# Lagging low-part products behind a norm, and a compression on both weight halves at once, in a two-block decoder on one core

## The reference, cut to what matters

```python
def rmsnorm(t, g):
    tf = tf * lax.rsqrt(jnp.mean(tf * tf, axis=-1, keepdims=True) + NORM_EPS)
...
h = rmsnorm(x, norm_mix[i]) * (1.0 + sc1) + sh1      # then h @ wqkv
h2 = rmsnorm(x, norm_ffn[i]) * (1.0 + sc2) + sh2     # then h2 @ ffn_up
...
def nsa_compress(k, pos_emb, w1, b1, w2, b2):
    nc = (T - NSA_CMP_LEN) // NSA_CMP_STRIDE + 1          # 15 blocks
    blocks = k[:, idx] + pos_emb
    flat = blocks.reshape(B, nc, NSA_CMP_LEN * hd)        # 15 x 2048
    return jax.nn.silu(flat @ w1 + b1) @ w2 + b2          # w1: 2048 x 128
```

## Time and profile before

| what | value |
|---|---|
| time, median of 3 runs | 1620.4 us (1619.64 to 1622.11) |
| the profiled execution's own time | 1614.25 us |
| its span, first to last instruction | 1612.1 us |
| granted TensorE clock, mean | 0.996 |
| PE, PEld busy | 98%, 83% |
| DVE, ACT, POOL busy | 59%, 48%, 34% |
| instructions | 24595 |
| matmul records of L731, one and two columns | 84 and 32 |
| DMA | 249.26 MB, 155 GB/s on average |

### The profile page before, as it was taken

The page is one execution under the profiler, slowest core; times in us unless marked ns, Lnnn a source line. Parts: engine busy times, 40 slices in busy tenths (PEclk is TensorE's granted clock), DMA queues, the critical chain, the costliest instruction groups (busy, mean ns, idle before and its releaser), DMA issues.

```text
span 1612.1 us, 24595 instructions
## 1 busy us (share of the span) xinstructions
PE 1584.4 (98%) x9838; PEld 1339.2 (83%) x9838; DVE 949.9 (59%) x1485; ACT 767.5 (48%) x1410; POOL 548.8 (34%) x358
## 2 busy tenths in 40 slices
PE   8999999999999999999999999999999999999998
PEld 5778557778887888879767999999999989999987
DVE  4334485555564653343275888658776567768545
ACT  5323585444322443243274755445544555564454
POOL 2224243322211222123172111016334567533564
PEclk9999999999999999999999999999999999999999
DMA  9264500434174222364314654445534544533451
GB/s 394 83 250 186 228 9 27 183 138 164 48 282 165 83 76 81 140 209 157 104 28 163 238 187 168 169 170 183 182 131 158 183 160 170 185 128 134 180 203 58
DMA packets 52464, 249.26 MB, mean 155 GB/s; under 512 B 20608, under 2 KB 20736, under 8 KB 25856
## 3 DMA queue, kind: packets, MB, share of 16 engines
q1 hardware_dynamic: 43600, 243.90, 41.9%
q10 hardware_dynamic: 8752, 3.80, 1.0%
HBM read 246.63 MB, written 1.05 MB: 154 GB/s over the span
## 4 chain that ended last, share of the span: by engine, by line
PE 89%; DVE 6%; ACT 2%; issue 1%; DMA 1%; POOL 0%; SPq 0%; ACTq 0%; POOLq 0%; DVEq 0%
PE psq L551 14%; PE psq L553 14%; PE psq L552 14%; PE psq L965 7%; PE ps L551 6%; PE ps L553 6%; PE ps L552 6%; PE psq L966 4%; PE ps L965 3%; PE ps L565 2%; PE ps L966 1%; DVE WL L533 1%; PE psq L1373 1%; PE ps L1401 1%; DMA RAW<-wstream 1%
## 5 line engine op out<-in xcount | busy, mean ns | idle before, releaser
L533 POOL TENSOR_TENSOR WL<-RAW,WH 128x1024 fp32r<-128x1024 f32 (+2 forms) x116 | 304.4, 2626 | 504.5 <-ACT WH L523 493.4
L533 DVE TENSOR_TENSOR WL<-RAW,WH 128x1024 fp32r<-128x1024 f32 (+3 forms) x264 | 329.2, 1272 | 235.6 <-ACT WH L523 235.4
L523 ACT ACTIVATE WH<-RAW 128x1024 fp32r<-128x1024 f32 (+2 forms) x380 | 361.0, 1001 | 156.2 <-DMA RAW<-wstream 92.5
L551 PE MATMUL psq<-NHL,WH 128*128 128x256 f32 (+1 forms) x1260 | 410.2, 326 | 3.3 <-POOL NHL L869 1.8
L553 PE MATMUL psq<-NHL,WL 128*128 128x256 f32 (+1 forms) x1260 | 404.3, 321 | 0.0
L552 PE MATMUL psq<-NHL,WH 128*128 128x256 f32 (+1 forms) x1260 | 404.2, 321 | 0.0
L551 PEld LDWEIGHTS psq<-NHL,WH 128*128 128x128 f32 x1260 | 239.9, 190 | 32.4 <-issue 7.6
L553 PEld LDWEIGHTS psq<-NHL,WL 128*128 128x128 f32 x1260 | 239.9, 190 | 17.8
L552 PEld LDWEIGHTS psq<-NHL,WH 128*128 128x128 f32 x1260 | 240.0, 191 | 16.6
L965 PE MATMUL psq<-NHL,WH 128*128 128x512 f32 x416 | 148.6, 400 | 0.0
L551 PE MATMUL ps<-NHL,WH 128*128 128x256 f32 (+1 forms) x368 | 122.1, 332 | 0.0
(11 more groups left out here) (398 smaller groups left out, 2871.0 us busy)
## 6 DMA issues: line engine op xcount, KB each, us to landing
RAW<-wstream SPq DMA_DIRECT2D x196, 1024.0 KB, 4.9
RAW<-wstream SPq DMA_DIRECT2D x32, 704.0 KB, 4.0
K<-first SPq DMA_DIRECT2D x4, 1024.0 KB, 17.1
X<-xin SPq DMA_DIRECT2D x2, 1024.0 KB, 6.3
V<-first SPq DMA_DIRECT2D x2, 1024.0 KB, 19.2
Q<-first SPq DMA_DIRECT2D x2, 1024.0 KB, 25.4
BR<-rpb ACTq DMA_DIRECT2D x8, 256.0 KB, 7.9
BR<-rpb SPq DMA_DIRECT2D x8, 256.0 KB, 8.6
```

What stands on the lines that cost most here:

```text
L523: e.activation(WH[:, u % 3, a:z], RAW[:, v % 3, a:z], ACT.Copy).then_inc(w_hi, 1)
L533: e.tensor_tensor(WL[:, u % 3, a:z], RAW[:, v % 3, a:z], WH[:, u % 3, a:z].bitcast(F32), ALU.subtract).then_inc(w_lo_p if pool else w_lo_v, 1)
L551: e.matmul(o, lh, rh, start=start, stop=False)
```

## The change

The sums over squares stream 64 equal columns (32 of each kind in the double norm) into 64 columns of NB, and dve_mean reads one of them. pe_high_first goes through all k: high products of tile k, then the low product of tile k-1; it replaces the abreast branch of pe_wide and the call of pe_tiles. In dve_head the split for "kf" moves ahead of the memset. WH and WL become two halves of one tensor, so that pe_compress_up can stream 256 columns, 128 high and 128 low, in one matmul; ACT copies 256 columns, and pe_compress_sum adds both halves. The computed values are the same sums in another order.

```diff
-        WH = sb("WH", [P, 3, UNIT], F32R)
-        WL = sb("WL", [P, 3, UNIT], F32R)
+        WHL = sb("WHL", [P, 2, 3, UNIT], F32R)
+        WH, WL = WHL[:, 0, :, :], WHL[:, 1, :, :]
...
-            width = 2 if n == 5 else 1
+            if n == 5:
+                kinds = GSQ[:, m, :].unsqueeze(2).to_broadcast([P, 2, 32])
+            else:
+                kinds = ONE.to_broadcast([P, 64])
             for q in range(NORM_T[n] // P):
-                mm = e.matmul(NB[:, width * q:width * q + width], t[:, q * P:q * P + P], GSQ[:, m, :] if n == 5 else ONE,
+                mm = e.matmul(NB[:, 64 * q:64 * q + 64], t[:, q * P:q * P + P], kinds,
                               start=first and q == 0, stop=m == DT - 1, skip_group_check=True)
...
         def pe_high_first(e, n, key, outs, T, shared):
             v, wh, wl = weights(key)
-            wait_weights(e, v, 0)
-            e.wait_ge(n_hi, split_base(n) + NORM_T[n] // 256)
-            for j, o in enumerate(outs):
-                w = slice(P * j, P * j + P)
-                e.matmul(o, wh[:, 0, w], NH[:, 0, 0:T], start=j == 0 or not shared, stop=False, skip_group_check=shared)
-                e.matmul(o, wl[:, 0, w], NH[:, 0, 0:T], start=False, stop=False, skip_group_check=shared)
-            pe_wait_norm(e, n, 0)
-            for j, o in enumerate(outs):
-                e.matmul(o, wh[:, 0, P * j:P * j + P], NL[:, 0, 0:T], start=False, stop=False, skip_group_check=shared)
+            H, base = NORM_T[n] // 256, split_base(n)
+            for k in range(DT + 1):
+                if k < DT:
+                    wait_weights(e, v, k)
+                    e.wait_ge(n_hi, base + H * k + H)
+                    for j, o in enumerate(outs):
+                        w = slice(P * j, P * j + P)
+                        e.matmul(o, wh[:, k, w], NH[:, k, 0:T], start=k == 0 and (j == 0 or not shared), stop=False,
+                                 skip_group_check=shared)
+                        e.matmul(o, wl[:, k, w], NH[:, k, 0:T], start=False, stop=False, skip_group_check=shared)
+                if k:
+                    pe_wait_norm(e, n, k - 1)
+                    for j, o in enumerate(outs):
+                        mm = e.matmul(o, wh[:, k - 1, P * j:P * j + P], NL[:, k - 1, 0:T], start=False, stop=k == DT,
+                                      skip_group_check=shared)
+                        if k == DT and (not shared or j == 1):
+                            mm.then_inc(gemm, 1)
...
+            lo_prep(e, l, "kf", False)
             e.memset(CM[:, 0:384].bitcast(U32), 0).then_inc(cm_zero, 1)
             dve_turn_product(e, l, 1)
-            lo_prep(e, l, "kf", False)
             dve_turn_sum(e, l, 1, KN[:, :, :])
...
-                v, wh, wl = weights(("cmp", l, kind))
+                v = UNIT_OF[("cmp", l, kind)]
+                both = WHL[:, :, SPLIT_AT[v] % 3, :].rearrange("p s (k n) -> p s k n", k=16)
                 for k in range(16):
-                    lhs = FHL[:, 512 * kind + 32 * k:512 * kind + 32 * k + P]
                     wait_weights(e, v, k)
-                    e.matmul(bank[6 + kind][:, 0:P], lhs, wh[:, k, :], start=k == 0, stop=False)
-                    mm = e.matmul(bank[6 + kind][:, 0:P], lhs, wl[:, k, :], start=False, stop=k == 15)
+                    mm = e.matmul(bank[6 + kind][:, 0:256], FHL[:, 512 * kind + 32 * k:512 * kind + 32 * k + P],
+                                  both[:, :, k, :], start=k == 0, stop=k == 15)
...
-                e.matmul(bank[6][:, 256 + 16 * kind:272 + 16 * kind], TMP[0:32, 3 + kind, 0:P],
-                         CONST[0:32, CO["sum16"]:CO["sum16"] + 16], start=True, stop=True).then_inc(cmp_mm, 1)
+                for half in range(2):
+                    mm = e.matmul(bank[6][:, 256 + 16 * kind:272 + 16 * kind],
+                                  TMP[0:32, 3 + kind, P * half:P * half + P],
+                                  CONST[0:32, CO["sum16"]:CO["sum16"] + 16], start=half == 0, stop=half == 1)
+                mm.then_inc(cmp_mm, 1)
```

More of the change, by code:

```diff
@@ L779, in dve_mean @@
                 for kind in range(2):
-                    mm = e.tensor_scalar(MS[:, 2 * kind:2 * kind + 2], NB[:, 0:4].rearrange("p (q s) -> p s q", s=2)[:, kind, :],
+                    mm = e.tensor_scalar(MS[:, 2 * kind:2 * kind + 2], NB[:, 32 * kind:32 * kind + 128:64],
                                          1.0 / D, EPS * EPS if kind == 0 else EPS, ALU.mult, ALU.add)
@@ L783, in dve_mean @@
                 return
-            e.tensor_scalar(MS[:, 0:nt], NB[:, 0:nt], 1.0 / D, EPS, ALU.mult, ALU.add).then_inc(ms_done, 1)
+            sums = NB[:, 0:nt] if n == 0 else NB[:, 0:64 * nt:64]
+            e.tensor_scalar(MS[:, 0:nt], sums, 1.0 / D, EPS, ALU.mult, ALU.add).then_inc(ms_done, 1)
         def rs_columns(n):
@@ L903, in pe_high_first, with pe_wide @@
             v, wh, wl = weights(key)
-            wait_weights(e, v, 0)
-            e.wait_ge(n_hi, split_base(n) + NORM_T[n] // 256)
-            for j, o in enumerate(outs):
-                w = slice(P * j, P * j + P)
-                e.matmul(o, wh[:, 0, w], NH[:, 0, 0:T], start=j == 0 or not shared, stop=False, skip_group_check=shared)
-                e.matmul(o, wl[:, 0, w], NH[:, 0, 0:T], start=False, stop=False, skip_group_check=shared)
-            pe_wait_norm(e, n, 0)
-            for j, o in enumerate(outs):
-                e.matmul(o, wh[:, 0, P * j:P * j + P], NL[:, 0, 0:T], start=False, stop=False, skip_group_check=shared)
-        def pe_wide(e, key, outs, T, xh, xl, wait_x, abreast=False):
+            H, base = NORM_T[n] // 256, split_base(n)
[15 more added lines that the diff above has]
+                            mm.then_inc(gemm, 1)
+        def pe_wide(e, key, outs, T, xh, xl, wait_x):
             v, wh, wl = weights(key)
             nk = SHAPE[v][0]
[L918 to L927, removed]
             for j, o in enumerate(outs):
@@ L1022, in pe_qkv @@
                         pe_ada_turn(e, 5)
-                wait_x = (lambda k: pe_wait_norm(e, n, k)) if u == 0 else nothing
                 if l == 1 and i < 4:
-                    pe_wide(e, ("qkv", l, i), [bank[b][:, 0:256], bank[b][:, 256:512]], 256, NH, NL, wait_x)
+                    pe_wide(e, ("qkv", l, i), [bank[b][:, 0:256], bank[b][:, 256:512]], 256, NH, NL, nothing)
                 else:
+                    outs = [bank[b][:, :], bank[b + 1][:, :]]
                     if u == 0:
-                        pe_high_first(e, n, ("qkv", l, i), [bank[b][:, :], bank[b + 1][:, :]], 512, False)
-                    pe_wide(e, ("qkv", l, i), [bank[b][:, :], bank[b + 1][:, :]], 512, NH, NL, wait_x, u == 0)
+                        pe_high_first(e, n, ("qkv", l, i), outs, 512, False)
+                    else:
+                        pe_wide(e, ("qkv", l, i), outs, 512, NH, NL, nothing)
                 if l == 0:
@@ L1605, in pe_ffn @@
                         e.wait_ge(x_res, 16 + 4 * jj + 8)
-                    wait_x = (lambda k: pe_wait_norm(e, 1 + 2 * l, k)) if j == 0 else nothing
                     outs = [b[:, :] for b in up_banks(l, jj)]
@@ L1622, in pe_ffn @@
                     if j == 0:
-                        pe_high_first(e, 1 + 2 * l, ("up", l, j), [bank[0][:, 0:256], bank[0][:, 256:512]] if l else outs, T, l == 1)
-                    if l == 1 and j == 0:
-                        pe_tiles(e, ("up", l, j), bank[0], (0, 1), range(1, DT), NH, NL, wait_x).then_inc(gemm, 1)
+                        pe_high_first(e, 1 + 2 * l, ("up", l, j), outs, T, l == 1)
                     else:
-                        pe_wide(e, ("up", l, j), outs, T, NH, NL, wait_x, j == 0)
+                        pe_wide(e, ("up", l, j), outs, T, NH, NL, nothing)
                 pe_down(e, l, c)
@@ L2094, in act_compress_up @@
                 e.wait_ge(gemm, product(("cmp", l, kind)))
-                e.activation(TMP[0:32, 3 + kind, 0:P], bank[6 + kind][0:32, 0:P],
+                e.activation(TMP[0:32, 3 + kind, 0:256], bank[6 + kind][0:32, 0:256],
                              ACT.Copy).then_inc(sb_copy, 1)
```

## The result

The changed kernel took 1607.2 us (median of 4 runs, 1605.91 to 1607.85) against 1620.02 us (4 runs, 1618.73 to 1622.11): ratio 0.9919, 95% interval 0.9901 to 0.9936, 12.8 us less. The forecast, 1613.8 us in a range from 1610.9, had the sign and half the size. The two profiled executions say something else: their spans are 1612.1 and 1605.7 us, only 6.4 us apart, close to the 6.6 us of the sum. So two questions stood: how the 6.4 us are made up, and where the other 6.4 come from.

What follows compares the result with a forecast made beforehand. TensorE, busy 98% of the span, was taken as the bound. Sums 2.2, lag 2.3, layer 1's head 2.1, layer 0's head 0.1, less 0.1, made 6.6 us: 1620.4 to 1613.8 us, range 1610.9 to 1618.2.

Steps and rivals of the forecast that it cites:

- the 6.6 us of the sum: Whole kernel: 2.2 + 2.3 + 2.1 + 0.1 - 0.1 us gained, taken off the 1620.4 us median.
- Rival 5: Layer heads: PE idles between thin stretches and its clock falls there; 3.6 us slower, 1624.0 us; chance 0.03.
- The head of layer 1: Earlier split removes a 1.9 us loss, wide products shorten each kind; net 2.1 us gained, other end 3.5.
- the dear order: Layer 1's head: POOL's split comes between DVE's next two, so g1's weights are ready at 1390.4, not 1388.3.
- rival 2: DVE keeps the port in both heads: 1.4 + 1.4 us more, 9.4 us gained, 1611.0 us; chance 0.08.
- The head of layer 0: Saved products turn into PE waiting; g1 0.3 us earlier, sums cost 0.2, net 0.1 us gained.
- the other end of the forecast: Layer 0's head: minus 0.9 us if POOL's split of cmp1 takes the port before the turn's sum.
- The lag: Three norms: lagging low products hide POOL's low parts; 0.8, 1.0 and 0.5 us, sum 2.3, ends 0 and 2.4.
- The wide sums: Norms: 64 columns cost nothing and keep the clock up; 1.1 us each at first and third, together 2.2 us.
- rival 1: Norms: the clock falls however many columns a sum streams; 4.4 us remain, 1616.0 us; chance 0.15.
- three signs of being wrong: Clock still falls behind the sums; L731's records further apart than 0.12 us; g1 of layer 0 starts later than before.

Runs made afterwards that it cites:

- early split alone: Kernel before with only DVE's split of cmp0 moved ahead of the memset and the turn's product; 128-column products kept: 1612.74 us, ratio 0.9964.
- products into the wait: Kernel before with 15 unused 256-column products added where PE stood 1.8 us in layer 1's head: 1614.29 us, ratio 0.9978.
- wide products alone: Kernel before with only the compression's products widened to 256 columns, 16 a kind; DVE's split left in place: 1614.96 us, ratio 0.9969.
- the change without the early split: Changed kernel with DVE's split of cmp0 put back behind the memset and the turn's product: 1611.81 us, ratio 0.9959.
- the fillers: Changed kernel with 7 and 6 unused 256-column products put into PE's two waits in layer 0's head: 1608.63 us, beside 1608.13 us.
- wide sums alone: Kernel before with only the sums over squares streaming 64 equal columns: 1620.3 us, ratio 1.0007.
- all but the wide sums: Changed kernel without the 64-column sums, so with lagging low parts, earlier split and 256-column products: 1608.39 us, ratio 0.993.
- the head alone: Kernel before with only the earlier split for kf and the compression's 256-column products: 1612.12 us, ratio 0.9959.
- kernel before once more: Kernel before, unchanged, profiled one more time: 1624.91 us, in the upper group.
- lag alone: Kernel before with only the lagging low parts, low product of tile k-1 behind the high products of tile k: 1612.14 us, ratio 0.9961.

## Why the prediction was wrong

**The base.** The step that failed is the second paragraph of the prediction: "It is 6.2 us under the median of the three runs, 1620.4 us. I take the difference off the median, since nothing in the change touches what lies outside the span." The 6.2 us do not lie outside the span. They are for the most part the clock in layer 1's head, a thing the change touches: a fall there lengthens the stage by 6.3 to 8.0 us in the five profiles that have it, and by the times 59 of 84 runs of the kernel before have it. (The start of the kernel varies too, by up to 3.1 us.) The one profiled execution was of the others. Rival 5's last sentence, "Before, the clock did not fall in the heads", was read from that one execution and is false for most. The sum was made on the lower group and subtracted from the upper.

**The head of layer 1.** "Net 2.1 us; the other end is 3.5" was mis-sized even in the profile: 3.3 us. DVE and POOL in the changed kernel's head, beside the earlier trace rows:

```profile
1377.28 1.21 DVE L533 TENSOR_TENSOR WHL<-RAW,WHL 128x1024 fp32r<-128x1024 f32 x1
...
1382.97 2.35 DVE L533 TENSOR_TENSOR WHL<-RAW,WHL 128x1024 fp32r<-128x1024 f32 x2
```

```profile
1378.97 2.41 POOL L533 TENSOR_TENSOR WHL<-RAW,WHL 128x1024 fp32r<-128x1024 f32 x1 [2.84 <-ACT WHL L523]
...
1383.51 4.07 POOL L533 TENSOR_TENSOR WHL<-RAW,WHL 128x1024 fp32r<-128x1024 f32 x1 [2.06 <-ACT WHL L523]
```

The moved split ends at 1378.49, before POOL's begins, as forecast: 1.21 us instead of 3.41. But I took the dear order for the next two, and DVE kept the port: both splits in 2.35 us while POOL's, issued in the first of them, took 4.07. That is rival 2 for this layer. The gate unit g1 starts at 1386.19 instead of 1392.81 us; 2.8 us of that were won ahead of the head, so the head brings 3.8 us (2.3 forecast), and 0.5 us are lost again behind g1. What is worth more in the median is the clock: removing the wait ended the fall (early split alone; products into the wait), and the wide products would have cut it to two stretches of 3.4 us by themselves (wide products alone; the change without the early split).

**The head of layer 0.** Forecast 0.1 us gained, found 0.4 lost. The port went as in the other end of the forecast, "if POOL's split of cmp1 ... takes the port before the turn's sum":

```profile
1119.62 2.88 DVE L1967 TENSOR_TENSOR KN<-KN,TMP 128x512 f32<-128x512 f32 x1
...
1122.81 4.52 DVE L533 TENSOR_TENSOR WHL<-RAW,WHL 128x1024 fp32r<-128x1024 f32 x2
```

```profile
1119.55 2.40 POOL L533 TENSOR_TENSOR WHL<-RAW,WHL 128x1024 fp32r<-128x1024 f32 x1 [4.13 <-ACT WHL L523]
```

DVE's turn sum stood behind POOL's split, 2.88 us instead of the 0.69 that the like instruction takes in layer 1. POOL had issued 0.07 us earlier. The Trainium skill (SBUF — State Buffer, section Who interferes with whom) gives the port to whichever issues first, and that agrees here; in layer 1, where DVE had its second split with POOL's already waiting, the row does not settle it.

But the price of that end, 0.9 us, did not come. The gate unit g1 starts at 1127.55 us, 3.26 us earlier than before, where what stands ahead of the head came 3.22 us earlier: it is not late at all. In the kernel before POOL's split had held DVE up too, one step later: the four small subtractions (L2047) took 2.59 us there and take 0.39 now. The 0.4 us are lost behind g1, at the sums over rows, of which the first line is the kernel before and the second the changed one:

```profile
1136.70 0.61 PE L2111 MATMUL ps<-CONST,TMP 32*128 32x16 f32 x4
```

```profile
1133.47 1.06 PE L2112 MATMUL ps<-CONST,TMP 32*128 32x16 f32 x8
```

A sum16 product is on fp32 operands and leaves two records, so two more products are four more records; the product behind them starts 0.99 us after the first record, where it was 0.54. "Two more sum16 products, 0.11 us each, cost 0.2" counted one record for each product: it is 0.45 us, in both heads.

Rival 5's fall in the thinned heads did happen, once, from 1124.2 us, in both profiles of the changed kernel; it lies under the wait for DVE's split and costs nothing, as the fillers showed.

**The lag.** Right in place and nearly in size: of what the three norms' stages gained some 2.1 us are left for the lag once the wide sums' 1.1 us at the first and at the third are taken off, and the times against the lower group give 2.7, for 2.3 forecast. That POOL's waits would not move elsewhere held: the earlier trace rows's L869 lines have no successor. In its place PE waits at most 0.7 us for ACT's high part (L848), which I had put at 0.1.

**The wide sums.** The mechanism held. In the five profiles with wide sums the clock never fell behind the sums of the first or third norm (none of ten places); in the eleven with thin ones it fell at 15 of 22. All five with wide sums began with a low clock of 10.2 us at the start; the three with thin ones that began so fell at five of six, so the start does not explain it. What it is worth is less sure. In profiles where both fall it was 2.2 us (wide sums alone) and 1.6 us (all but the wide sums); with falls at 15 of 22 places that makes an estimate of 1.1 to 1.5 us on average, and no median here tells it from nothing. As the mechanism goes, rival 1 is out. By the rule in the Trainium skill (TensorE: Matmul & The Clock Gate, section Why this matters for your kernels), to avoid idle gaps between bursts, filling gapless sums mends nothing: the trace disagrees there. In layer 1's head, where a gap was the cause, it agrees in kind only: the gap of 1.8 us is shorter than those that section of the Trainium skill warns of.

**The range** took in the likelier of the ways that I had named, each within the profiled execution. None of the three signs of being wrong came. No rival was "the profile is not of a typical run", though 1614.25 against 1619.64 to 1622.11 us said just that.

Not settled: whether and why the place of the head in the run sets how often the clock falls behind the wait, why wide sums alone had all ten runs high, and what the further falls of 3.4 us in three profiles with wide products come from (1398.9 us with the head alone, 1138.0 and 1400.9 us with wide products alone, 1397.0 us without the early split). All four start 2.5 to 2.9 us behind the first sum16 product, among narrow products, and the change makes that stretch 0.45 us longer; no run tested it. No version tried here was faster than the changed kernel.

## What to carry to other kernels

When the profiled execution is faster than every timed run, it may have skipped something the others pay for, as here: take several profiles, compare span with span, and look for the granted clock before you take a wait list for the price list. A short wait of TensorE ahead of a thin stream can cost more than its length: fill it, remove it, or make the stream behind it wide. And before you mend a low clock, ask what PE waits for next; where another engine sets the next start, the slower products are free.

## What the runs showed of the hardware

- After PE had stood for 1.8 us, the clock was at 0.5 from 0.3 us (kernel before once more) to 2.7 us (lag alone: from 1384.6 to 1387.3) into the 128-column fp32r products, in all five profiles of the upper group, to which 59 of 84 timed runs belong. During them it did not come back: stretches of 13.6 and 17.1 us at 0.5 with PE busy throughout. With 256-column products it came back after 3.4 us (wide products alone; the change without the early split), and fell once more.
- At 0.5 a 128-column product came every 0.21 instead of 0.11 us, and 16 of 256 columns took 3.67 instead of 1.98 us.
- The same program had the clock low in its first 30 us for 3.4, 6.8 or 10.2 us (three profiles of the kernel before), 3.1 us of span apart.
- Behind sums of one column, in the first profile after 3.80 us of PE busy without a gap, the clock fell at 15 of 22 places; behind the same sums over 64 columns at none of 10.
- A sum16 product (fp32, 16 columns) leaves two records, some 0.11 us each: 0.45 us for two.
- Work added (15 products) took 5 us off the median, and 2.3 us of work added elsewhere put 8 us on it.
